# What is moved: the first MLP matmul steps into the pooling mixer, by a generator

## The chip, the cores and the metric

The kernel runs on all 8 cores of one Trainium2 chip, the same program on each: core i takes prompt sequence i (2048 tokens) and 16 of the 128 running sequences (16 x 8 = 128 tokens). No core talks to another. The metric is the device time in microseconds of the slowest core. Each core has TensorE (PE, matmuls into PSUM), VectorE (DVE), ScalarE (ACT), GpSimd (POOL) and SyncE (SP); here POOL and SP issue the DMAs. Every engine works through its own instruction list in the order in which the program wrote it, and waits on semaphores where an operand is not ready.

## The reference, cut to what matters

```python
def trunk(x, c, pool_buf, pos0, ...):
    for i in range(2):                                   # layer 0: pooling mixer, layer 1: spatial gating
        sh1, sc1, g1, sh2, sc2, g2 = split(silu(c) @ w_ada[i] + b_ada[i])     # w_ada[i] is 1024 x 6144
        h = rms_norm(x, norm_g[i, 0]) * (1 + sc1) + sh1
        if i == 0: y, nb = pool_mixer(h, buf, pos0, w_pool, pool_scale)
        else:      y, vr = sgu_mixer(h, ...)
        x = x + g1 * y
        h = rms_norm(x, norm_g[i, 1]) * (1 + sc2) + sh2
        a = relu(h @ mlp_w1[i])                          # 1024 -> 4096
        x = x + g2 * ((a * a) @ mlp_w2[i])               # 4096 -> 1024
    return rms_norm(x, final_g), ...

def pool_mixer(h, buf, ...):
    # four channel groups of 256, windows w = 2, 4, 8, 16:
    # mean of the last w tokens minus the token, then a 256 x 256 map per group, then a scale
    d = mean_w(h) - h
    return einsum('blgc,gcd->blgd', d, w_pool) * pool_scale
```

x is float32, matmul operands are bfloat16.

## The kernel before

Everything is kept transposed, channels on the 128 partitions: x (`xT_sb`) as 8 channel chunks by 2176 tokens in float32 and the normalised h (`hT_sb`) in bfloat16, both whole in SBUF. The tokens are cut into five groups: 0 to 3 are 512 prompt tokens each, group 4 is the 128 sample tokens.

Weights come through a ring of six 128 x 4096 bfloat16 buffers. The list of pieces is fixed: 12 pieces of `w_ada` of layer 0, 12 of layer 1, then for the MLP of layer 0 `w1` and `w2` of block 0, of block 1, and so on (8 blocks of 512 hidden channels). Piece i is loaded by a DMA that POOL issues (L267) as soon as piece i-6 has been used up for the last time.

The stages that matter here, in the order of the program:

- **Front.** Layer 0's modulation (`ada_piece(0, a)`: 32 small matmuls into `psM` and four ACT copies each), and the first norm of the five groups.
- **Pooling mixer**, group by group. DVE builds the eight window sums `dT` of a group (L543 to L564; for group 4 L572 to L586). `mid_group` then puts in the second norm of the group before it: ACT squares x (L350), PE adds the squares up over the channels with a matrix of ones (L353, called the statistics below), DVE and ACT make rstd (L358 to L363), DVE scales x into h (L383), ACT adds the shift (L387). Then come the matmuls of the map, 32 for a group of 512 tokens (L597, L604) into the three banks `psB`, and eight DVE additions into x (L431; L437 and L440 for group 4). After each group `pm_after` uses up three `w_ada` pieces of layer 1, so pieces 9 to 11 come after group 3.
- **MLP of layer 0.** 40 steps, (block, group), blocks outside. `mm1(i)` is 32 matmuls into the three banks `psA` (L459), each bank followed on ACT by relu and square into `aT` (L465, L467). `mm2(i)` is 32 matmuls from `aT` into `psB` (L484) and eight DVE additions into x (L431, or L437 and L440). The order is mm1(0), mm1(1), mm2(0), mm1(2), mm2(1), mm1(3), ... The second norms of groups 3 and 4 are put in behind mm1(0) and mm1(1).
- **Spatial gating and the MLP of layer 1** follow. The gating stage holds three small constants in buffers of their own: `wsp`, `binv`, `btile`.

The window sums of the pooling mixer live in the same two buffers `aT` as the hidden activations of the MLP. A step of the MLP is a pass of the loop in `mlp`; below, step i means mm1(i) followed by mm2(i-1), and "ada pieces" are those of `w_ada`.

Of the kernel before, what the change touches and what calls it, by code (L numbers as in the profile page):

```python
# [134 lines left out]
def build_program():  # L135
# [481 lines left out]
    def sgu_setup():  # L617
        w32 = scr.ap()[:, 0:1024].rearrange("p (g k t) -> p g k t", g=4, k=2)
        m32 = scr.ap()[:, 1024:1280].rearrange("p (k t) -> p k t", k=2)
        S.add("sp", lambda e: e.dma_start(out=w32, in_=d_wsp.ap()), writes=[SCR(0, 4096)], stream="s_wsp")  # L620
# [4 lines left out]
        S.add("pool", lambda e: e.dma_start(out=binv.ap(), in_=d_binv.ap()), writes=[("binv", 0, 1)], stream="s_binv")

    def sgu(after_sub=None, lazy=()):
        l = 1
# [17 lines left out]
        for g, (t0, n) in enumerate(GROUPS):
            c0, _ = hcols(g)
            sample = (g == 4)
# [80 lines left out]
            for cc in range(NDC):
                gi = cc // 2  # L730
                bank, bkey = banks4[nxt("A4", 4)]
                for tt in range(ntile):
# [182 lines left out]
```

How the kernel before makes its waits and increments, by code:

```python
                def body(eng, ops=self.ops[e], e=e):  # L105
                    waited = {}
                    for op in ops:
                        need = {}
                        for d in op.deps:
                            sem, val = d.sigval
                            k = id(sem)
                            if k not in need or need[k][1] < val:
                                need[k] = (sem, val)
                        for k, (sem, val) in need.items():
                            if waited.get(k, 0) >= val:
                                continue
                            eng.wait_ge(sem, val)
                            waited[k] = val
                        ins = op.emit(eng)
                        if op.stream is not None:
                            ins.then_inc(op.sigval[0], 16)
                        elif op.signal:
                            ins.then_inc(op.sigval[0], 1)
                    if e == "sp":
                        for s, (sem, val) in final.items():
                            if waited.get(id(sem), 0) < val:
                                eng.wait_ge(sem, val)
                        for e2 in ENGS:
                            if e2 != e and ecount[e2] > 0:
                                eng.wait_ge(esem[e2], ecount[e2])
```

## Time and profile before

| | us |
|---|---|
| median of 2 runs | 1690.68 (1689.95 to 1691.41) |
| the profiled execution, its own time | 1690.05 |
| its span on core 0, the slowest | 1688.5 |
| spans of the other cores | 1681.3 to 1686.4 |
| PE busy / DVE busy / ACT busy in the span | 1332.7 / 880.4 / 596.0 |

The profile is one execution, recorded on the slowest core. The time around the span is 1690.05 - 1688.5 = 1.55 us. Positions such as "221.49" are microseconds from the start of the span. A matmul of 512 columns is one that streams a group of 512 tokens. A row of the timeline merges neighbouring instructions of one kind ("x31") and gives start and length; what stands in square brackets is the idle time of the engine before it and what ended it. Some matmul records are missing, so that 32 may read as 31.

### The profile page before, as it was taken

The numbers are of one execution on the slowest core, as the hardware profiler recorded it, in microseconds if no ns is written. First come the engines' busy times: TensorE is split into PE (matmuls) and PEld (weight loads), VectorE is DVE, ScalarE is ACT, GpSimd is POOL, SyncE is SP. The second block draws the span as 40 slices with busy tenths as digits, with TensorE's granted clock in tenths as the row PEclk, the third lists the DMA queues.
The fourth block names the chain that finished last, engine by engine and source line by source line (L and its number), as shares of the span: only waits on it lengthen the run. The fifth ranks groups of instructions, "written<-read, shape, count | busy, mean of one in ns | idle before, by whom it ended". The sixth has DMA issues, their size and how long they took to land.

```text
span 1688.5 us, 22112 instructions; the slowest of 8 cores (1681.3 to 1688.5 us)
## 1 busy us (share of the span) xinstructions
PE 1332.7 (79%) x7190; PEld 623.5 (37%) x7314; DVE 880.4 (52%) x1695; ACT 596.0 (35%) x1221; POOL 65.2 (4%) x86
## 2 busy tenths in 40 slices
PE   0233666999999999986888877638999999999982
PEld 0111232444444444432333323323444444444431
DVE  0247775544544435448566466546453544444478
ACT  0450544233233343344412605314334333333352
POOL 2010110000000000000000000000000000000000
PEclk9955777999999999999888978768999999999996
DMA  9999984033123113111200000090311311300023
GB/s 200 200 159 143 144 121 70 1 50 42 20 41 51 25 27 51 26 26 26 57 1 0 1 1 13 7 162 1 51 26 26 51 26 26 51 1 1 1 85 129
DMA packets 75055, 90.05 MB, mean 53 GB/s; under 512 B 4400, under 2 KB 57904, under 8 KB 74928
## 3 DMA queue, kind: packets, MB, share of 16 engines
q0 software_dynamic: 58400, 66.30, 28.0%
q1 hardware_dynamic: 16544, 22.33, 4.4%
q8 instruction: 63, 1.03, 0.3%
q14 instruction: 48, 0.39, 0.1%
HBM read 144.36 MB, written 11.01 MB: 92 GB/s over the span
## 4 chain that ended last, share of the span: by engine, by line
PE 64%; DVE 19%; issue 7%; ACT 4%; DMA 4%; another core or an unknown queue 2%; DVEq 1%; POOL 0%; ACTq 0%; POOLq 0%; SPq 0%
PE psA L459 26%; PE psB L484 26%; PE psB L750 4%; DVE hT_sb L383 4%; DMA ring<-w_ada 3%; PE psS L353 2%; DVE scr L437 2%; DVE xT_sb L440 1%; DVE hT_sb L391 1%; PE psA L659 1%; DVE xT_sb L373 1%; DVE psA L740 1%; DMA btile<-bsp_pack 1%; PE psA L673 1%
## 5 line engine op out<-in xcount | busy, mean ns | idle before, releaser
L431 DVE SCALAR_TENSOR_TENSOR xT_sb<-psB,modT,xT_sb 128x512 f32<-128x512 f32 x544 | 406.1, 750 | 361.0 <-PE psB L484 302.7
L484 PE MATMUL psB<-aT,ring 128*128 128x512 bf16 (+1 forms) x2510 | 500.5, 351 | 59.2 <-DVE scr L437 43.1
L459 PE MATMUL psA<-hT_sb,ring 128*128 128x512 bf16 (+1 forms) x2513 | 485.6, 349 | 9.3 <-ACT aT L465 6.6
L465 ACT ACTIVATE aT<-psA 128x512 bf16<-128x512 f32 (+1 forms) x320 | 169.6, 530 | 608.8 <-PE psA L459 608.6
L484 PEld LDWEIGHTS psB<-aT,ring 128*128 128x128 bf16 x2560 | 233.3, 99 | 315.7 <-issue 80.4
L459 PEld LDWEIGHTS psA<-hT_sb,ring 128*128 128x128 bf16 x2560 | 230.8, 98 | 252.1 <-issue 13.6
L467 ACT ACTIVATE aT<-aT 128x512 bf16<-128x512 bf16 (+1 forms) x320 | 181.1, 566 | 30.4 <-ACT aT L465 1.5
L350 ACT ACTIVATE sq<-xT_sb 128x512 bf16<-128x512 f32 (+1 forms) x200 | 95.3, 558 | 110.7 <-PE psS L353 78.6
L353 PE MATMUL psS<-sq,ones 128*128 128x512 bf16 (+1 forms) x193 | 73.8, 436 | 46.8 <-ACT sq L350 40.9
L295 PE MATMUL psM<-siluT,ring 128*128 128x17 bf16 x768 | 23.5, 173 | 100.5 <-DMA ring<-w_ada 78.9
L383 DVE SCALAR_TENSOR_TENSOR hT_sb<-xT_sb,modT,rstd 128x512 bf16<-128x512 f32 x128 | 92.5, 745 | 9.1 <-ACT rstd L363 9.0
L437 DVE TENSOR_TENSOR scr<-psB,modT 128x128 f32<-128x128 f32 x136 | 39.7, 292 | 103.4 <-PE psB L484 91.2
L750 PE MATMUL psB<-aT,ring 128*128 128x512 bf16 (+1 forms) x312 | 78.8, 415 | 10.9 <-DVE aT L742 9.8
L302 ACT ACTIVATE modT<-psM,vecs_sb 128x17 f32<-128x17 f32 x96 | 18.4, 274 | 140.2 <-PE psM L295 140.2
L597 PE MATMUL psB<-aT,aux4k 128*128 128x512 bf16 (+1 forms) x79 | 29.0, 464 | 48.5 <-DVE xT_sb L431 22.6
L358 DVE TENSOR_SCALAR rstd<-psS 128x512 f32<-128x512 f32 (+1 forms) x25 | 15.2, 608 | 93.6 <-PE psS L353 93.6
L659 PE MATMUL psA<-hT_sb,ring 128*128 128x512 bf16 (+1 forms) x267 | 56.3, 364 | 8.4 <-ACT scr L679 8.0
L295 PEld LDWEIGHTS psM<-siluT,ring 128*128 128x128 bf16 x768 | 22.2, 100 | 103.6 <-issue 102.6
L673 PE MATMUL psA<-ring,hT_sb 128*128 128x512 bf16 x173 | 44.9, 404 | 14.7 <-ACT scr L679 14.4
L353 PEld LDWEIGHTS psS<-sq,ones 128*128 128x128 bf16 x200 | 19.9, 101 | 98.5 <-issue 93.9
L267 POOL DMA_DIRECT2D ring<-mlp_w x32 | 26.9, 840 | 740.0 <-PE psA L459 448.0
L750 PEld LDWEIGHTS psB<-aT,ring 128*128 128x128 bf16 x320 | 34.2, 116 | 54.3 <-issue 34.0
(90 smaller groups left out, 706.4 us busy)
## 6 DMA issues: line engine op xcount, KB each, us to landing
ring<-mlp_w POOLq DMA_DIRECT2D x32, 1024.0 KB, 11.0
ring<-w_ada POOLq DMA_DIRECT2D x24, 1024.0 KB, 42.1
xT_sb<-xT SPq DMA_DIRECT2D x4, 2048.0 KB, 40.9
yT<-xT_sb SPq DMA_DIRECT2D x32, 256.0 KB, 2.0
ring<-sgu_w_in POOLq DMA_DIRECT2D x4, 1024.0 KB, 10.8
ring<-sgu_w_out POOLq DMA_DIRECT2D x2, 1024.0 KB, 13.6
hT_sb<-spT POOLq DMA_DIRECT2D x1, 736.0 KB, 83.7
aux4k<-w_pool POOLq DMA_DIRECT2D x1, 512.0 KB, 77.3
```

What stands on the lines that cost most here:

```text
L350: S.add("act", lambda e, si=si, dc=dc, t0=t0, n=n: e.activation(out=sq[si].ap()[:, 0:n], in_=xT.ap()[:, dc, t0:t0 + n], func=AF.Square), r ...
L353: S.add("pe", lambda e, si=si, dc=dc, n=n: e.matmul(psS.ap()[:, 0:n], ones.ap(), sq[si].ap()[:, 0:n], start=(dc == 0), stop=(dc == NDC - 1 ...
L383: S.add("dve", lambda e, hs=hs, xs=xs, R=R, dc=dc: e.scalar_tensor_tensor(out=hs, in0=xs, scalar=modT.ap()[:, l, DER[vA], dc, 0:1], in1=R, ...
L431: S.add("dve", lambda e: e.scalar_tensor_tensor(out=xs, in0=ps_ap, scalar=modT.ap()[:, l, DER[kG], dout_c, 0:1], in1=xs, op0=ALU.mult, op1 ...
L437: S.add("dve", lambda e: e.tensor_tensor(out=tmp, in0=ps_ap.rearrange("p (b t) -> p b t", t=8), in1=bc_seq(modT.ap(), l, DER[kG], dout_c), ...
L459: S.add("pe", lambda e, pso=pso, wv=wv, dc=dc, fc=fc, c0=c0, n=n: e.matmul(pso, wv[:, dc, fc * 128:(fc + 1) * 128], hT.ap()[:, dc, c0:c0 + n],
L465: S.add("act", lambda e, av=av, pso=pso: e.activation(out=av, in_=pso, func=AF.Relu), reads=[(("psA", bi), 0, 512)], writes=areg)
L467: S.add("act", lambda e, av=av: e.activation(out=av, in_=av, func=AF.Square), reads=areg, writes=areg)
L484: S.add("pe", lambda e, pso=pso, wv=wv, dc=dc, fc=fc, n=n, ab=ab: e.matmul(pso, wv[:, fc, dc * 128:(dc + 1) * 128], aT[ab].ap()[:, fc, 0:n ...
L659: S.add("pe", lambda e, pso=pso, wv=wv, dc=dc, fc=fc: e.matmul(pso, wv[:, dc, (fc % 4) * 128:(fc % 4 + 1) * 128], hT.ap()[:, dc, c0:c0 + n ...
L673: S.add("pe", lambda e, pso=pso, wv=wv, dc=dc, c0=c0, tt=tt: e.matmul(pso, hT.ap()[:, dc, c0 + tt * 128:c0 + (tt + 1) * 128], wv[:, dc, :] ...
L750: S.add("pe", lambda e, pso=pso, wv=wv, dco=dco, cc=cc, uT=uT: e.matmul(pso, wv[:, cc, (dco % 4) * 128:(dco % 4 + 1) * 128], uT[cc], start ...
```

## The change

`mlp` becomes a generator, `mlp_gen`, that yields after each step. It is made before the pooling mixer, and steps of it are drawn in `pm_after`: two behind group 2 (mm1(0); mm1(1) and mm2(0)), one behind group 3 (mm1(2) and mm2(1)), one behind group 4 (mm1(3) and mm2(2)); then comes the second norm of group 4, and then the rest. The second norm of group 3 goes to the middle of group 4 of the mixer, with its shift on ACT. So that window sums and hidden activations can be alive together, the window sums get a buffer of 128 x 4096 bfloat16 of their own, `l1buf`, which later holds `wsp`, `binv` and `btile`.

```diff
-    wsp = sb("wsp", [128, 4, 2, 128], BF16)
-    btile = sb("btile", [128, 4, 128], F32)
-    binv = sb("binv_sb", [1, D], BF16)
+    l1buf = sb("l1buf", [128, 4096], BF16)
...
+    wsp = _V(lambda: l1buf.ap()[:, 0:1024].rearrange("p (g k t) -> p g k t", g=4, k=2))
+    binv = _V(lambda: l1buf.ap()[0:1, 1024:2048])
+    btile = _V(lambda: l1buf.ap()[:, 2048:3072].bitcast(F32).rearrange("p (g t) -> p g t", t=128))
...
-    def mlp(l, after_blk=None, after_last=None, lazy=(), flush=True):
+    def mlp_gen(l, after_blk=None, after_last=None, lazy=(), flush=True):
...
                 mm2(i - 1)
+            yield i
...
-        dT = [aT[0].ap()[:, i, :] for i in range(4)] + [aT[1].ap()[:, i, :] for i in range(4)]
+        dT = [l1buf.ap()[:, i * 512:(i + 1) * 512] for i in range(8)]
...
+    gen0 = mlp_gen(0, after_blk=mlp0_after_blk, after_last=lambda g, part: norm_group(1, 0, g, part=part), lazy=[], flush=False)
+
     def pm_mid(g):
-        if 1 <= g <= 3:
+        if 1 <= g <= 4:
             norm_group(0, 1, g - 1, shift_eng="act")
 
     def pm_after(g):
         for _ in range(3):
             if ada1:
                 ada_piece(1, ada1.pop(0))
+        if g == 2:
+            next(gen0)
+            next(gen0)
+        if g == 3:
+            next(gen0)
...
-    tail0 = mlp(0, after_blk=mlp0_after_blk, after_last=lambda g, part: norm_group(1, 0, g, part=part),
-                lazy=[lambda: norm_group(0, 1, 3), lambda: norm_group(0, 1, 4)], flush=False)
+    next(gen0)
+    norm_group(0, 1, 4)
+    tail0 = run_gen(gen0)
```

What this does to the order on DVE, between groups 2 and 3 of the mixer. Before (L431 is the addition into x, L543 and L549 begin the window sums of group 3):

```order
L358 TENSOR_SCALAR rstd<-psS 128x512
L383 SCALAR_TENSOR_TENSOR hT_sb<-xT_sb,modT,rstd 128x512 x8
L431 SCALAR_TENSOR_TENSOR xT_sb<-psB,modT,xT_sb 128x512 x8
L543 TENSOR_TENSOR aT<-hT_sb 128x512 x2
L549 TENSOR_TENSOR scr<-hT_sb 128x527
```

Now, at the same place (the lines have moved: L439 is the addition, L562 and L568 begin the window sums):

```order
L366 TENSOR_SCALAR rstd<-psS 128x512
L391 SCALAR_TENSOR_TENSOR hT_sb<-xT_sb,modT,rstd 128x512 x8
L439 SCALAR_TENSOR_TENSOR xT_sb<-psB,modT,xT_sb 128x512 x16
L562 TENSOR_TENSOR l1buf<-hT_sb 128x512 x2
L568 TENSOR_TENSOR scr<-hT_sb 128x527
```

The eight additions of mm2(0) stand behind the eight of group 2 and ahead of the window sums of group 3. The same holds behind group 3, with those of mm2(1).

On PE, from the last matmuls of the map of group 3 on. Before (L295 are the ada pieces, L353 the statistics, L459 mm1, L484 mm2):

```order
L604 MATMUL psB<-hT_sb,scr 128x512 x2
L295 MATMUL psM<-siluT,ring 128x17 x96
L597 MATMUL psB<-aT,aux4k 128x128 x16
L459 MATMUL psA<-hT_sb,ring 128x512 x32
L353 MATMUL psS<-sq,ones 128x512 x8
L459 MATMUL psA<-hT_sb,ring 128x512 x32
L353 MATMUL psS<-sq,ones 128x128 x8
L484 MATMUL psB<-aT,ring 128x512 x32
L459 MATMUL psA<-hT_sb,ring 128x512 x32
L484 MATMUL psB<-aT,ring 128x512 x32
L459 MATMUL psA<-hT_sb,ring 128x512 x32
```

Now (L303 the ada pieces, L361 the statistics, L467 mm1, L492 mm2, L616 and L623 the map):

```order
L623 MATMUL psB<-hT_sb,scr 128x512 x2
L303 MATMUL psM<-siluT,ring 128x17 x96
L467 MATMUL psA<-hT_sb,ring 128x512 x32
L492 MATMUL psB<-aT,ring 128x512 x32
L361 MATMUL psS<-sq,ones 128x512 x8
L616 MATMUL psB<-l1buf,aux4k 128x128 x16
L467 MATMUL psA<-hT_sb,ring 128x512 x32
L492 MATMUL psB<-aT,ring 128x512 x32
L361 MATMUL psS<-sq,ones 128x128 x8
L467 MATMUL psA<-hT_sb,ring 128x128 x32
L492 MATMUL psB<-aT,ring 128x512 x32
```

Here mm1(2) and mm2(1) stand ahead of the map of group 4, mm1(3) and mm2(2) behind it, and the statistics of group 4 directly ahead of mm1(4), which is the first matmul step that reads group 4. mm1(0), mm1(1) and mm2(0) stand further up, behind the ada pieces of group 2.

The lists of POOL and SP keep their order: POOL issues the same ring pieces in the same sequence.

## Rows read from the trace of the kernel before

**Rows 1.** Busy time by stretch, core 0: busy us (x instructions) of each engine, granted PE clock, DMA share, GB/s

```profile
200.00:240.00 40.00, 23.16 (x156) 9.71 (x159) 31.99 (x61) 24.44 (x52) 3.38 (x4) 0.76 0.99 131
240.00:280.00 40.00, 28.03 (x188) 12.30 (x189) 21.36 (x70) 14.07 (x33) 2.39 (x3) 0.73 0.74 110
560.00:700.00 140.00, 135.71 (x707) 65.14 (x720) 66.36 (x108) 48.30 (x88) 3.39 (x4) 1.00 0.22 31
220.00:341.00 121.00, 88.36 (x545) 40.51 (x551) 74.10 (x172) 44.53 (x102) 5.80 (x7) 0.82 0.42 57
```

**Rows 2.** Timeline of PE, ada pieces behind groups 2 and 3, map of group 4, mm1(0)

```profile
223.92 0.99 PE L295 MATMUL psM<-siluT,ring 128*128 128x17 bf16 x32 [1.01 <-ACT modT L302]
246.32 0.96 PE L295 MATMUL psM<-siluT,ring 128*128 128x17 bf16 x32
250.25 0.95 PE L295 MATMUL psM<-siluT,ring 128*128 128x17 bf16 x32 [1.01 <-ACT modT L302]
261.11 8.87 PE L459 MATMUL psA<-hT_sb,ring 128*128 128x512 bf16 x31 [0.22 <-issue]
```

**Rows 3.** Timeline of DVE from the window sums of group 3 to those of group 4

```profile
220.92 0.75 DVE L543 TENSOR_TENSOR aT<-hT_sb 128x512 bf16<-128x512 bf16 x2
230.98 0.69 DVE L358 TENSOR_SCALAR rstd<-psS 128x512 f32<-128x512 f32 x1
238.52 2.06 DVE L431 SCALAR_TENSOR_TENSOR xT_sb<-psB,modT,xT_sb 128x512 f32<-128x512 f32 x3
247.26 0.38 DVE L572 TENSOR_TENSOR aT<-hT_sb 128x128 bf16<-128x128 bf16 x2
256.92 0.28 DVE L437 TENSOR_TENSOR scr<-psB,modT 128x128 f32<-128x128 f32 x1
```

**Rows 4.** Timeline, statistics of group 4 to the restart of mm2(0), DVE and PE

```profile
284.90 1.55 PE L353 MATMUL psS<-sq,ones 128*128 128x128 bf16 x8 [1.87 <-ACT sq L350]
287.45 0.28 DVE L358 TENSOR_SCALAR rstd<-psS 128x128 f32<-128x128 f32 x1
288.64 0.29 DVE L399 TENSOR_TENSOR rstd<-xT_sb,modT 128x128 f32<-128x128 f32 x1 [0.91 <-ACT rstd L363]
297.95 2.06 DVE L431 SCALAR_TENSOR_TENSOR xT_sb<-psB,modT,xT_sb 128x512 f32<-128x512 f32 x3
298.84 3.57 PE L484 MATMUL psB<-aT,ring 128*128 128x512 bf16 x8 [8.44 <-DVE xT_sb L431]
```

**Rows 5.** Timeline, the MLP at its pace: steps 2 to 5

```profile
305.06 7.07 PE L459 MATMUL psA<-hT_sb,ring 128*128 128x512 bf16 x32
311.96 7.07 PE L484 MATMUL psB<-aT,ring 128*128 128x512 bf16 x31
313.10 6.79 DVE L431 SCALAR_TENSOR_TENSOR xT_sb<-psB,modT,xT_sb 128x512 f32<-128x512 f32 x8 [7.02 <-PE psB L484]
318.87 7.07 PE L459 MATMUL psA<-hT_sb,ring 128*128 128x512 bf16 x31
332.68 1.95 PE L459 MATMUL psA<-hT_sb,ring 128*128 128x128 bf16 x32
334.68 6.85 PE L484 MATMUL psB<-aT,ring 128*128 128x512 bf16 x31
341.38 7.07 PE L459 MATMUL psA<-hT_sb,ring 128*128 128x512 bf16 x31
```

**Rows 6.** Timeline of POOL: issues of the ring pieces w1(0), w2(0), later w1(3)

```profile
221.49 0.88 POOL L267 DMA_DIRECT2D ring<-mlp_w  x1 [20.33 <-PE psM L295]
223.45 0.75 POOL L267 DMA_DIRECT2D ring<-mlp_w  x1 [1.09 <-PE psM L295]
335.18 0.90 POOL L267 DMA_DIRECT2D ring<-mlp_w  x1 [82.67 <-PE psA L459]
```

**Rows 7.** DMA view, issue to landing (last number, us): the pieces issued at 221.49, 223.45, 335.18

```profile
ring<-mlp_w POOLq DMA_DIRECT2D x1, 1024.0 KB, 15.0
ring<-mlp_w POOLq DMA_DIRECT2D x1, 1024.0 KB, 19.3
ring<-mlp_w POOLq DMA_DIRECT2D x1, 1024.0 KB, 11.6
```

More of the change, by code:

```diff
@@ L185, in build_program, with __init__, ap @@
     siluT = sb("siluT", [128, NDC, NSEQ], BF16)
-    wsp = sb("wsp", [128, 4, 2, 128], BF16)
-    btile = sb("btile", [128, 4, 128], F32)
-    binv = sb("binv_sb", [1, D], BF16)
+    l1buf = sb("l1buf", [128, 4096], BF16)
+    class _V:
+        def __init__(self, f):
+            self.f = f
+        def ap(self):
+            return self.f()
+    wsp = _V(lambda: l1buf.ap()[:, 0:1024].rearrange("p (g k t) -> p g k t", g=4, k=2))
+    binv = _V(lambda: l1buf.ap()[0:1, 1024:2048])
+    btile = _V(lambda: l1buf.ap()[:, 2048:3072].bitcast(F32).rearrange("p (g t) -> p g t", t=128))
     lnst = sb("lnst", [128, 16], F32)
@@ L514, in mlp, with run_gen @@
         return rest_
+    def run_gen(gen):
+        try:
+            while True:
+                next(gen)
+        except StopIteration as e_:
+            return e_.value
+    def mlp(*a_, **k_):
+        return run_gen(mlp_gen(*a_, **k_))
     def pool_mixer(after_group=None, mid_group=None):
@@ L524, in pool_mixer @@
                   reads=[("aux4k", 0, 1)], writes=[SCR(8320 + k_ * 512, 8320 + (k_ + 1) * 512)])
-        dT = [aT[0].ap()[:, i, :] for i in range(4)] + [aT[1].ap()[:, i, :] for i in range(4)]
-        dreg = [[(("aT", 0), i * 512, (i + 1) * 512)] for i in range(4)] + [[(("aT", 1), i * 512, (i + 1) * 512)] for i in range(4)]
+        dT = [l1buf.ap()[:, i * 512:(i + 1) * 512] for i in range(8)]
+        dreg = [[("l1buf", i * 1024, (i + 1) * 1024)] for i in range(8)]
         for g, (t0, n) in enumerate(GROUPS):
@@ L623, in sgu_setup @@
             S.add("dve", lambda e, gi=gi: e.tensor_tensor(out=wsp.ap()[:, gi, :, :], in0=w32[:, gi, :, :], in1=m32, op=ALU.mult),
-                  reads=[SCR(0, 5120)], writes=[("wsp", gi, gi + 1)])
-        S.add("pool", lambda e: e.dma_start(out=binv.ap(), in_=d_binv.ap()), writes=[("binv", 0, 1)], stream="s_binv")
+                  reads=[SCR(0, 5120)], writes=[("l1buf", gi * 512, (gi + 1) * 512)])
+        S.add("pool", lambda e: e.dma_start(out=binv.ap(), in_=d_binv.ap()), writes=[("l1buf", 2048, 4096)], stream="s_binv")
     def sgu(after_sub=None, lazy=()):
@@ L644, in sgu @@
         S.add("sp", lambda e: e.dma_start(out=btile.ap(), in_=bass.AP(d_bsp, 0, [[0, 128], [256, 4], [1, 128]])),
-              writes=[("btile", 0, 1)], stream="s_bt")
+              writes=[("l1buf", 4096, 6144)], stream="s_bt")
         for g, (t0, n) in enumerate(GROUPS):
@@ L677, in sgu @@
                                                                    start=False, stop=True),
-                          reads=[("ones", 0, 1), ("binv", 0, 1)], writes=[(bkey, 0, 512)])
+                          reads=[("ones", 0, 1), ("l1buf", 2048, 4096)], writes=[(bkey, 0, 512)])
                     S.add("act", lambda e, pso=pso, hf=hf: e.activation(out=vst[:, hf * 512:(hf + 1) * 512], in_=pso, func=AF.Gelu,
@@ L727, in sgu @@
                 S.add("sp", lambda e: e.dma_start(out=btile.ap(), in_=bass.AP(d_bsp, 128, [[0, 128], [256, 4], [1, 128]])),
-                      writes=[("btile", 0, 1)], stream="s_bt")
+                      writes=[("l1buf", 4096, 6144)], stream="s_bt")
             for cc in range(NDC):
@@ L735, in sgu @@
                         pso, vtm[:, tt, cc * 128:(cc + 1) * 128], wsp.ap()[:, gi, kk, :], start=True, stop=True),
-                        reads=[SCR(tt * 2048, (tt + 1) * 2048), ("wsp", gi, gi + 1)], writes=[(bkey, 0, 512)])
+                        reads=[SCR(tt * 2048, (tt + 1) * 2048), ("l1buf", gi * 512, (gi + 1) * 512)], writes=[(bkey, 0, 512)])
                 bt = btile.ap()[:, gi, :]
@@ L740, in sgu @@
                 S.add("dve", lambda e, p3=p3, btb=btb: e.tensor_tensor(out=p3, in0=p3, in1=btb, op=ALU.add),
-                      reads=[(bkey, 0, 512), ("btile", 0, 1)], writes=[(bkey, 0, 512)])
+                      reads=[(bkey, 0, 512), ("l1buf", 4096, 6144)], writes=[(bkey, 0, 512)])
                 S.add("dve", lambda e, bank=bank, cc=cc, n=n, uT=uT: e.tensor_tensor(
@@ L813, in build_program, with mlp0_after_blk @@
     ada1 = list(range(12))
+    def mlp0_after_blk(blk):
+        if blk == 6:
+            sgu_setup()
+    gen0 = mlp_gen(0, after_blk=mlp0_after_blk, after_last=lambda g, part: norm_group(1, 0, g, part=part), lazy=[], flush=False)
     def pm_mid(g):
-        if 1 <= g <= 3:
+        if 1 <= g <= 4:
             norm_group(0, 1, g - 1, shift_eng="act")
@@ L829, in build_program @@
     ada_derive_G2(1)
-    def mlp0_after_blk(blk):
-        if blk == 6:
-            sgu_setup()
-    tail0 = mlp(0, after_blk=mlp0_after_blk, after_last=lambda g, part: norm_group(1, 0, g, part=part),
-                lazy=[lambda: norm_group(0, 1, 3), lambda: norm_group(0, 1, 4)], flush=False)
+    next(gen0)
+    norm_group(0, 1, 4)
+    tail0 = run_gen(gen0)
     tail1 = sgu(after_sub=lambda g, part: norm_group(1, 1, g, part=part), lazy=tail0)
```

## The prediction, made blind

> **What bounds the kernel now.** I first read busy time by stretch [rows 1]. From 560 to 700 us the MLP keeps PE busy 135.7 of 140 us at the full clock (1.00, the level of 2.4 GHz): there PE is the bound, nothing of the change touches it, and every microsecond that the MLP starts later goes to the end. From 200 to 280 us it is otherwise: PE 23.2 and 28.0 of 40, DVE 32.0 and 21.4, PE clock 0.76 and 0.73. The engines take turns there. So the change works on a stretch with idle time on PE, some 121 us from 220 to 341, in which PE works 88.4 us and DVE 74.1. Whether the idle time is filled or only moved is then a question of order, and I followed the timeline of DVE and PE through this stretch.
>
> Before, the window sums of group 3 start on DVE at 220.92, its rstd at 230.98, its additions into x at 238.52, and the window sums of group 4 at 247.26 [rows 3]: 26.3 us for a group, of which nearly all is DVE work. MLP step 0 starts on PE at 261.11 [rows 2]. mm2(0) is held up by the second norms of groups 3 and 4 on DVE, restarts at 298.84 after 8.44 us of idle PE [rows 4], and from 305.06 on PE is fed without a gap: mm1(2) 305.06, mm2(1) 311.96, mm1(3) 318.87, mm1(4) 332.68, mm2(3) 334.68, mm1(5) 341.38 [rows 5]. A half step of 512-token width is thus 6.9 us. **The anchor is the start of mm1(5)**, 341.38: from there on both programs are the same, so the shift of this instant is the answer.
>
> **The change, walked through.** The weights decide the first term. w1(0) can only be issued when ada piece 6 of layer 1 is used up; POOL issues it at 221.49 and it lands 15.0 us later, at 236.5 [rows 6, 7]. The last ada piece in front of mm1(0) ends on PE at 224.9 [rows 2]. Before, this landing was hidden: mm1(0) came at 261. Now PE waits from 224.9 to 236.5, 11.6 us. Bounds: the same kind of piece issued alone lands in 11.6 us [rows 7], which would give 233.1; the middle piece of the trio takes 19.3, which would give 240.8. I take 15.0, since the same three pieces go out at the same instants with the same neighbours.
>
> 1. mm1(0) begins after a pause of PE. The same step before took 8.87 us, against 7.07 at the full clock [rows 2, 5]; I take 8.7 start to start: 236.5 to 245.2. mm1(1): 6.9, to 252.1. mm2(0) starts at 252.1 (w2(0), landed at 223.45 + 19.3 = 242.8, is there).
> 2. DVE. Its order says: eight additions of group 2, then eight of mm2(0), then the window sums of group 3. An undisturbed mm2 gives DVE its first bank 1.14 us after PE begins and the eighth addition ends 7.93 us after (311.96, 313.10 + 6.79) [rows 5]. So DVE idles from 220.9 to 253.2, 32.3 us, and is free at 260.0. This is the wait that takes the place of the idle PE: behind it stand the window sums, rstd and the scaling of group 2's norm, and everything of group 3.
> 3. Group 3 takes the 26.3 us it took before: window sums of group 4 would be next at 286.3. Its statistics are on PE by then. PE starts the three ada pieces 0.9 us ahead of that, as before (246.32 against 247.26), and needs 4.9 us (246.32 to 251.2) [rows 2, 3]: 290.3.
> 4. mm1(2) to 297.2, mm2(1) from there, DVE free at 305.1. DVE idled from 286.3 to 298.3 for it.
> 5. Window sums of group 4: 256.92 - 247.26 = 9.7 us, to 314.8. Norm of group 3: 238.52 - 230.98 = 7.5 us, to 322.3. Then the additions of group 4; PE gets to its next step 4.2 us after they begin (261.11 - 256.92), at 326.5 [rows 2, 3].
> 6. mm1(3), after another pause of PE, 8.7 us to 335.2; mm2(2) to 342.1; DVE free at 343.1.
> 7. Norm of group 4, which mm1(4) now waits for with nothing in between. The squares are ready; the statistics, in order on PE behind mm2(2), take about 1.5 us, to 343.6. From rstd to the first scaling 1.2 us, the 24 small operations 297.95 - 288.64 = 9.3 us: 354.2 [rows 4]. mm1(4) runs along, and finishes its other three banks 1.5 us later (2.0 us for four banks, [rows 5]): 355.7. **PE idles some 11 us** here; before, the same 9.3 us of DVE held mm2(0) for 8.4, so this wait isn't taken away but moved.
> 8. mm2(3) 6.7 us, with up to 2 us for a clock that has fallen in the pause: mm1(5) at 362.4 to 364.4.
>
> Against 341.38 that is 21.0 to 23.0 later, **+22 us**. Smaller edits: the shift of group 3's norm goes to ACT and saves DVE eight operations, already in the 7.5 us of step 5. The generator itself and the views into `l1buf` add no instruction. `l1buf` makes `wsp`, `binv` and `btile` wait for the map of group 4, which is over hundreds of microseconds before they are written: nothing, and nothing also if that cover were thinner, as POOL and SP issue them at the same places in their queues. The mask DMA on SP, which waits for the last window sums, slides with them and is needed only from block 6.
>
> The bounds of what the rows of before do not fix, the landing and the restarts of PE at half clock (1.8 us each in steps 1, 6 and 8): 22 - 3.4 - 3 x 1.8 = 13 below, and above, with the late landing and a restart at mm1(2) as well, 22 + 4.3 + 1.8 = 28.
>
> The time goes against the profiled execution: 1690.05 + 22 = 1712. The median of the runs shown, 1690.68, is 0.6 above it, which I leave in the range.
>
> A rule to weigh at the landing. In the rows, w1(0) takes 15.0 us to land while DVE works on bfloat16 sums, and 11.6 us much later, alone in the queue. The Trainium skill (SBUF — State Buffer, section "Who interferes with whom") says that DVE in its two-port modes locks GpSimd out of the port by which it writes the descriptors of its DMAs. Read loosely, an idle DVE would let w1(0) land 3.4 us sooner and the sum would be 18.6. The same section excepts tensor_tensor, which is nearly all that DVE does between 221 and 231, so by the rule as it stands nothing changes.
>
> **Rivals.**
>
> *Early landing.* The trio lands faster beside an idle DVE: 1690.05 + 22 - 3.4 = 1709. For it: DVE is the only thing that changes beside the DMAs. Against: three pieces share the queue either way. It is inside the forecast's own range. With the three restarts at full clock as well the cost is the lower bound, 13: 1703.
>
> *The overlap pays after all (not slower).* One mechanism, at DVE's wait of 32.3 us in step 2: if DVE did group 3's 26.3 us in that gap, and not behind it, the time would be 1712 - 26.3 = 1686, and with the 12 us of step 4 used as well 1674. It decides as soon as 22 us of the two gaps are used. For it: PE's 88.4 us of work in 121 leave room [rows 1], and this is the form the interleaving would need. Against: the order of DVE has the additions of mm2(0) in front of the window sums, and DVE works in order.
>
> *PE stays at half clock.* If the moved half steps all ran at the level of 1.2 GHz, each would take 13.8 us and not 6.9. For the five that I put at full clock (mm1(1), mm2(0), mm1(2), mm2(1), mm2(2)) that is 5 x 6.9 = 34 us more, 1746. Half of it gives 1729, slower by 2.3%. For it: granted clock 0.76 and 0.73 here [rows 1]. Against: mm1(0) itself, after a pause, lost only 1.8 us.
>
> *The change does not do what it says.* The order shows it does; no chance set aside.
>
> **How the numbers follow.** Forecast, 1706 to 1718: 0.75. A lesser cost, 1692 to 1706 (early landing together with short restarts, or a shorter group 3): 0.12. Not slower: 0.04. More than 1718: 0.09, of which above 1724.5 (the +2% line) 0.04. What a measurement of this kernel can tell from no change is about 2%, 34 us; the forecast is 1.3%, so it lies within. The range that should hold the time 8 times in 10 reaches a little below and above the forecast's own: 1703 to 1721. Faster by over 2% (under 1657) needs both gaps used and more: 0.02. Slower by over 2%: 0.04. Within: 0.94.
>
> **What would show it.** In the changed kernel: PE idle between the ada pieces and mm1(0) with w1 as releaser, 11 to 12 us, ending near 236.5; the largest single wait of DVE, some 32 us, at the addition into x, released by a matmul of mm2; the window sums of group 3 near 260, of group 4 near 305; a wait of PE at mm1(4) of 128 columns of about 10 us for h; mm1(5) near 363. The step most apt to fail is the third: if group 3 takes less than 26.3 us because its statistics and matmuls are ready sooner, the cost falls by that much. What would prove it wrong: a mm1(5) before 350, or another stage, behind 350 us, that gains or loses more than 3 us.

## The result, and the profile after

| | before | changed |
|---|---|---|
| median, us | 1690.68, with the later runs 1691.98 | 1715.01 |
| profiled execution, us | 1690.05 | 1712.89 |
| span of its slowest core | 1688.5 (core 0) | 1711.3 (core 3) |
| start of mm1(5) of layer 0 on that core | 341.38 | 364.98 |

The ratio is 1.0135, 95% interval 1.012 to 1.015: slower by 1.35%. Ratios, here and below, leave out the runs in which half of the chip, or all of it, showed a lower granted clock; the medians include them (up to 1844.7 and 1893.7 us here). The forecast was 1712, range 1703 to 1721.

Busy time by stretch on core 3 of the changed kernel, columns as in [rows 1]:

```profile
220.00:341.00 121.00, 74.72 (x446) 33.80 (x447) 57.20 (x128) 47.01 (x97) 4.89 (x6) 0.79 0.37 54
365.00:420.00 55.00, 53.27 (x292) 25.84 (x291) 23.58 (x42) 21.03 (x38) 0.75 (x1) 1.00 0.12 20
```

PE works 74.7 us between 220 and 341 where it worked 88.4, DVE 57.2 where it worked 74.1 [rows 1]. Less is done in the same stretch on both engines, so they wait more, for each other and for weights. From 365 us on PE is at the full clock and nearly always busy, as before.

Some waits between 221 and 363 us, in total, number, longest:

```profile
DVE xT_sb L439 <- PE psB L492: 55.9, 11, 31.2
PE psA L467 <- DMA ring<-mlp_w: 10.2, 1, 10.2
PE psA L467 <- DVE hT_sb L424: 9.0, 8, 2.5
PE psB L616 <- DVE scr L445: 16.7, 5, 14.7
PE psB L616 <- DVE xT_sb L439: 14.2, 1, 14.2
```

The first is DVE at its additions for a bank of mm2, the second PE for w1(0), the third PE at mm1(4) for h of group 4. These are the three waits of the walk. The last two are the other side of the first: PE stands in front of the map of groups 3 and 4 (L616) for 14 us each time, because DVE, freed late from the additions of mm2, has yet to do the norm and to empty the banks. Now the timeline. PE, behind the ada pieces of group 2:

```profile
234.01 16.18 PE L467 MATMUL psA<-hT_sb,ring 128*128 128x512 bf16 x64 [10.18 <-DMA ring<-mlp_w]
250.02 7.07 PE L492 MATMUL psB<-aT,ring 128*128 128x512 bf16 x32
```

PE idles 10.18 us for the ring and starts the two mm1 at 234.01 (before, the first of them came at 261.11 [rows 2]). DVE through groups 3 and 4:

```profile
251.16 6.79 DVE L439 SCALAR_TENSOR_TENSOR xT_sb<-psB,modT,xT_sb 128x512 f32<-128x512 f32 x8 [31.23 <-PE psB L492]
257.87 0.75 DVE L562 TENSOR_TENSOR l1buf<-hT_sb 128x512 bf16<-128x512 bf16 x2
270.15 5.39 DVE L391 SCALAR_TENSOR_TENSOR hT_sb<-xT_sb,modT,rstd 128x512 bf16<-128x512 f32 x8 [1.55 <-ACT rstd L371]
275.46 2.06 DVE L439 SCALAR_TENSOR_TENSOR xT_sb<-psB,modT,xT_sb 128x512 f32<-128x512 f32 x3
297.50 0.75 DVE L439 SCALAR_TENSOR_TENSOR xT_sb<-psB,modT,xT_sb 128x512 f32<-128x512 f32 x1 [13.45 <-PE psB L492]
305.33 0.38 DVE L591 TENSOR_TENSOR l1buf<-hT_sb 128x128 bf16<-128x128 bf16 x2
317.24 5.39 DVE L391 SCALAR_TENSOR_TENSOR hT_sb<-xT_sb,modT,rstd 128x512 bf16<-128x512 f32 x8 [1.56 <-ACT rstd L371]
```

DVE stands still for 31.23 us and then does the additions of mm2(0) at 251.16; only behind them, at 257.87, come the window sums of group 3, which stood at 220.92 before [rows 3]. The second insertion costs it 13.45 us (297.50), and the window sums of group 4 begin at 305.33 against 247.26 [rows 3]. PE again, steps 2 to 5:

```profile
287.78 8.75 PE L467 MATMUL psA<-hT_sb,ring 128*128 128x512 bf16 x32
296.37 8.19 PE L492 MATMUL psB<-aT,ring 128*128 128x512 bf16 x32
326.67 8.21 PE L467 MATMUL psA<-hT_sb,ring 128*128 128x512 bf16 x32
334.71 7.07 PE L492 MATMUL psB<-aT,ring 128*128 128x512 bf16 x32
345.54 0.22 PE L467 MATMUL psA<-hT_sb,ring 128*128 128x128 bf16 x1 [2.54 <-DVE hT_sb L424]
...
353.86 2.83 PE L467 MATMUL psA<-hT_sb,ring 128*128 128x128 bf16 x25 [0.92 <-DVE hT_sb L424]
356.47 8.66 PE L492 MATMUL psB<-aT,ring 128*128 128x512 bf16 x32
364.98 7.07 PE L467 MATMUL psA<-hT_sb,ring 128*128 128x512 bf16 x32
```

mm1(4) of 128 columns runs one matmul for each channel chunk that DVE finishes, from 345.54 to 353.86, and mm1(5) follows at 364.98; in [rows 5] it stood at 341.38. That is 23.6 us later, and the spans differ by 22.8. This sets the slowest core of one profile against the slowest of the other. Core against core, mm1(5) comes 12.7 (core 0) to 28.1 us (core 7) later, 19.9 on average, and the rest of the span behind it changes by -8.9 to +4.5 us, -2.1 on average. Such differences are scatter as far as can be told: on core 1 the same rest differs by 6.8 us between the kernel before and the one below that has only the new buffer. So behind the anchor nothing of weight changed, but agreement to 1 us is more than one profile can show.

### The profile page after: what moved, and what is told of

Read it like the earlier page. It is cut to its first block, busy times and chain, and to the rows that moved or that the text cites. A ratio compares the mean times of both kernels' runs of the same rounds, so it can differ in the third digit from the quotient of the medians.

```text
span 1711.3 us, 22257 instructions; the slowest of 8 cores (1693.4 to 1711.3 us)
## 1 busy us (share of the span) xinstructions
PE 1346.8 (79%) x7314; PEld 626.3 (37%) x7314; DVE 877.7 (51%) x1687; ACT 602.9 (35%) x1229; POOL 65.1 (4%) x86
## 3 DMA queue, kind: packets, MB, share of 16 engines
q0 software_dynamic: 58400, 66.30, 26.7%
## 4 chain that ended last, share of the span: by engine, by line
PE 68%; DVE 16%; issue 6%; DMA 4%; ACT 3%; another core or an unknown queue 1%; DVEq 1%; POOL 0%; ACTq 0%; SPq 0%; POOLq 0%
PE psA L467 27%; PE psB L492 26%; PE psB L769 4%; DVE hT_sb L391 3%; DMA ring<-w_ada 2%; PE psS L361 2%; PE psA L678 2%; PE psA L692 2%; DVE scr L445 2%; DVE xT_sb L448 1%; DVE xT_sb L381 1%; DVE psA L759 1%; DMA l1buf<-bsp_pack 1%; PE psM L692 1%
## 5 line engine op out<-in xcount | busy, mean ns | idle before, releaser
L439 DVE SCALAR_TENSOR_TENSOR xT_sb<-psB,modT,xT_sb 128x512 f32<-128x512 f32 x544 | 406.3, 750 | 399.8 <-PE psB L492 342.1
L492 PE MATMUL psB<-aT,ring 128*128 128x512 bf16 (+1 forms) x2560 | 504.2, 351 | 46.4 <-DVE scr L445 43.0
L467 PE MATMUL psA<-hT_sb,ring 128*128 128x512 bf16 (+1 forms) x2560 | 496.9, 353 | 25.8 <-DMA ring<-mlp_w 10.2
L492 PEld LDWEIGHTS psB<-aT,ring 128*128 128x128 bf16 x2560 | 233.2, 99 | 304.1 <-issue 69.6
L467 PEld LDWEIGHTS psA<-hT_sb,ring 128*128 128x128 bf16 x2560 | 233.5, 99 | 276.5 <-issue 43.2
L361 PE MATMUL psS<-sq,ones 128*128 128x512 bf16 (+1 forms) x200 | 72.8, 425 | 39.1 <-ACT sq L358 31.3
L303 PE MATMUL psM<-siluT,ring 128*128 128x17 bf16 x768 | 23.6, 173 | 98.4 <-DMA ring<-w_ada 76.3
L616 PE MATMUL psB<-l1buf,aux4k 128*128 128x512 bf16 (+1 forms) x80 | 29.5, 461 | 66.7 <-DVE xT_sb L439 30.8
L678 PE MATMUL psA<-hT_sb,ring 128*128 128x512 bf16 (+1 forms) x272 | 56.7, 365 | 8.0 <-ACT scr L698 8.0
L303 PEld LDWEIGHTS psM<-siluT,ring 128*128 128x128 bf16 x768 | 22.3, 100 | 101.7 <-issue 100.7
L366 DVE TENSOR_SCALAR rstd<-psS 128x512 f32<-128x512 f32 (+1 forms) x25 | 15.2, 608 | 81.7 <-PE psS L361 81.7
L361 PEld LDWEIGHTS psS<-sq,ones 128*128 128x128 bf16 x200 | 19.7, 101 | 90.0 <-issue 84.3
```

The lines of the kernel that those rows point to most:

```text
L361: S.add("pe", lambda e, si=si, dc=dc, n=n: e.matmul(psS.ap()[:, 0:n], ones.ap(), sq[si].ap()[:, 0:n], start=(dc == 0), stop=(dc == NDC - 1 ...
L439: S.add("dve", lambda e: e.scalar_tensor_tensor(out=xs, in0=ps_ap, scalar=modT.ap()[:, l, DER[kG], dout_c, 0:1], in1=xs, op0=ALU.mult, op1 ...
L467: S.add("pe", lambda e, pso=pso, wv=wv, dc=dc, fc=fc, c0=c0, n=n: e.matmul(pso, wv[:, dc, fc * 128:(fc + 1) * 128], hT.ap()[:, dc, c0:c0 + n],
L492: S.add("pe", lambda e, pso=pso, wv=wv, dc=dc, fc=fc, n=n, ab=ab: e.matmul(pso, wv[:, fc, dc * 128:(dc + 1) * 128], aT[ab].ap()[:, fc, 0:n ...
L678: S.add("pe", lambda e, pso=pso, wv=wv, dc=dc, fc=fc: e.matmul(pso, wv[:, dc, (fc % 4) * 128:(fc % 4 + 1) * 128], hT.ap()[:, dc, c0:c0 + n ...
```

## The experiments

All times are medians; a ratio is to the kernel before on the same chip, with its 95% interval. The theory (A) is that the time is lost by order alone: weights that have not landed, DVE held by the additions of an inserted step, and PE held by norm 4. Against it stood: the new buffer costs something; the landing wait only replaces another; the half clock of PE sets the stretch; DVE is the bound of the mixer, so that no interleaving can gain.

**Own buffer only.** The steps are no longer drawn into the mixer.

```diff
-        if 1 <= g <= 4:
+        if 1 <= g <= 3:
             norm_group(0, 1, g - 1, shift_eng="act")
...
-        if g == 2:
-            next(gen0)
-            next(gen0)
-        if g == 3:
-            next(gen0)
...
-    next(gen0)
-    norm_group(0, 1, 4)
-    tail0 = run_gen(gen0)
+    tail0 = mlp(0, after_blk=mlp0_after_blk, after_last=lambda g, part: norm_group(1, 0, g, part=part),
+                lazy=[lambda: norm_group(0, 1, 3), lambda: norm_group(0, 1, 4)], flush=False)
```

> The changed kernel with its own buffer for the window sums, but with no step drawn into the mixer (order as before). Theory A (order: the time is lost because DVE and PE wait for each other at the inserted steps): the buffer costs nothing, 1690 to 1692 us, mm1(5) of layer 0 near 341 us. Rival B (the shared buffer and its new dependencies, or other addresses, cost something of their own): 1695 to 1713 us.

1690.73 us, ratio 0.998 (0.996 to 1.001). PE, core 1:

```profile
260.30 9.30 PE L467 MATMUL psA<-hT_sb,ring 128*128 128x512 bf16 x32
340.98 7.07 PE L467 MATMUL psA<-hT_sb,ring 128*128 128x512 bf16 x32
```

The steps stand where they stood in [rows 2, 5], within 1 us. The buffer is free within the interval, and rival B is out: the loss lies in where the steps and the norms of groups 3 and 4 stand. (That the norm of group 3 moved along, with its shift on ACT, was not tested by itself.)

**Weights that have landed.** mm1(0), mm1(1) and mm2(0) read w_ada pieces 11 and 10, which have been in the ring for long. They multiply by the wrong weights, so the kernel's output is not the reference's; only its times are read.

```diff
+            if l == 0 and si < 2:
+                p1 = pidx[("ada", 1, 11)]
+                wv = pview(p1)
...
+            if l == 0 and si < 1:
+                p2 = pidx[("ada", 1, 10)]
+                wv = ring[p2 % NS].ap()[:, 0:4096].rearrange("p (a b) -> p a b", b=1024)
```

> The changed kernel, but mm1(0), mm1(1) and mm2(0) of layer 0 read ring pieces of w_ada that have landed long before (so the product of these steps is not the reference's); same instructions, same order. Theory A with the landing as its first term: mm1(0) starts at 225 us right behind the ada pieces on every core, the wait of 10 us for the ring is gone, the restart at half clock too; on the slowest core mm1(5) moves from 365 to about 353 and the time is 1701 us (1697 to 1704). Rival C (the landing only takes the place of another wait, PE being held up elsewhere anyway): at most 3 us better than the changed kernel, 1710 to 1715.

1704.01 us, ratio 1.007 (1.005 to 1.009): 11.0 less than the changed kernel, where 14 were expected. There are only four runs, and three of them took 1701.67, 1701.87 and 1706.16 us, so the 11 is good to some 4 us. PE, core 0 (the mm1 are L470 here, mm2 L498):

```profile
223.54 14.92 PE L470 MATMUL psA<-hT_sb,ring 128*128 128x512 bf16 x62 [0.23 <-issue]
238.30 7.07 PE L498 MATMUL psB<-aT,ring 128*128 128x512 bf16 x32
351.97 7.07 PE L470 MATMUL psA<-hT_sb,ring 128*128 128x512 bf16 x31
```

mm1(0) starts at 223.54, with no wait in front, and mm1(5) at 351.97, as walked (353). The median came out at the upper edge of the range. So the landing is worth some 11 us on the slowest core: a real term, and not another wait in disguise (rival C is out). Averaged over the cores it is less: mm1(0) starts 7.4 us earlier than in the changed kernel (224.5 against 231.8), and mm1(5) 7.4 us earlier too. What is left, 12 us over before, must come from the order behind it; the next runs take that apart.

**Norm 4 ahead of step 3.**

```diff
-    next(gen0)
     norm_group(0, 1, 4)
+    next(gen0)
     tail0 = run_gen(gen0)
```

> The changed kernel with the second norm of group 4 put ahead of step 3 and not behind it. Theory A: mm1(3) starts about 5 us later because the statistics stand in front of it, but the 24 small DVE operations run beside mm1(3) and PE no longer idles at mm1(4); mm1(5) about 9 us earlier than in the changed kernel, near 355, time 1704 to 1707. Rival D (the wait is only moved to mm2(2), as it stood at mm2(0) before the change): no more than 3 us better, 1710 to 1715.

1705.42 us, ratio 1.0085 (1.0065 to 1.0105): 9.6 less than the changed kernel. PE, core 6:

```profile
331.50 1.91 PE L467 MATMUL psA<-hT_sb,ring 128*128 128x512 bf16 x4
339.90 2.75 PE L492 MATMUL psB<-aT,ring 128*128 128x512 bf16 x12
344.99 6.03 PE L492 MATMUL psB<-aT,ring 128*128 128x512 bf16 x19 [2.33 <-DVE xT_sb L439]
350.86 1.95 PE L467 MATMUL psA<-hT_sb,ring 128*128 128x128 bf16 x32
359.55 7.07 PE L467 MATMUL psA<-hT_sb,ring 128*128 128x512 bf16 x31
```

mm1(4) comes at 350.86 in one piece, without the trickle. Rival D is out, since more than 3 us were gained, but it is right in a small part: mm2(2) waits 2.33 us for DVE, which ends norm 4 at 344.1. Here core 6 got its weights late (mm1(0) at 238.8), so mm1(5) at 359.55 and not 355.

**Draws behind the window sums.**

```diff
     def pm_mid(g):
+        if g == 3:
+            next(gen0)
+            next(gen0)
+        if g == 4:
+            next(gen0)
         if 1 <= g <= 4:
             norm_group(0, 1, g - 1, shift_eng="act")
...
-        if g == 2:
-            next(gen0)
-            next(gen0)
-        if g == 3:
-            next(gen0)
```

> The changed kernel with the steps drawn one place later: step 0 and 1 behind the window sums of group 3 (not ahead of them), step 2 behind those of group 4. Theory A (DVE's waits of 31 and 13 us at the additions of mm2 hold up the window sums): the sums, 10 us each, now lie in the gaps; PE's order and the landing stay as they are. 8 to 9 us less at each place, mm1(5) near 348, time 1695 to 1699. Rival E (it is PE's late start and its half clock that set the stretch, and DVE's order doesn't matter): within 3 us of the changed kernel.

1699.46 us, ratio 1.0044 (1.0034 to 1.0054): 15.6 less, half a us above the range expected, with PE's order of half steps as it was and the landing too (on this core PE waits 11.67 us for w1(0) and starts mm1(0) at 234.74). DVE, core 0:

```profile
219.07 0.75 DVE L562 TENSOR_TENSOR l1buf<-hT_sb 128x512 bf16<-128x512 bf16 x2
251.79 6.80 DVE L439 SCALAR_TENSOR_TENSOR xT_sb<-psB,modT,xT_sb 128x512 f32<-128x512 f32 x8 [22.57 <-PE psB L492]
262.58 5.39 DVE L391 SCALAR_TENSOR_TENSOR hT_sb<-xT_sb,modT,rstd 128x512 bf16<-128x512 f32 x8 [1.55 <-ACT rstd L371]
289.92 6.78 DVE L439 SCALAR_TENSOR_TENSOR xT_sb<-psB,modT,xT_sb 128x512 f32<-128x512 f32 x8 [3.78 <-PE psB L492]
300.69 5.39 DVE L391 SCALAR_TENSOR_TENSOR hT_sb<-xT_sb,modT,rstd 128x512 bf16<-128x512 f32 x8 [1.54 <-ACT rstd L371]
```

The window sums of group 3 start at 219.07, inside the gap, and the longest wait falls from 31.23 to 22.57 us, the second from 13.45 to 3.78. The scaling of norm 2 comes at 262.58 where it came at 270.15, that of norm 3 at 300.69 where it came at 317.24. Rival E is out: DVE's order does matter, some 8 us per place.

**Each draw one group later.**

```diff
-        if g == 2:
+        if g == 3:
             next(gen0)
-            next(gen0)
-        if g == 3:
             next(gen0)
...
+    next(gen0)
     next(gen0)
     norm_group(0, 1, 4)
```

> The changed kernel with every draw one group later: steps 0 and 1 behind group 3, steps 2 and 3 behind group 4, then the second norm of group 4. The weights have landed by then. Theory A: no wait for the ring; DVE still waits 19 us for mm2(0) behind group 3 (two mm1 and a bank after 252 us) and PE still idles 11 us at mm1(4); mm1(5) near 345 us, time 1694 to 1697. Rival C (the landing is not what the draw behind group 2 costs, each inserted step costs the same wherever it stands): 1705 or more.

1696.84 us, ratio 1.0031 (1.0017 to 1.0045). PE, core 6:

```profile
254.45 15.66 PE L467 MATMUL psA<-hT_sb,ring 128*128 128x512 bf16 x64
298.77 9.00 PE L467 MATMUL psA<-hT_sb,ring 128*128 128x512 bf16 x32
332.26 0.22 PE L467 MATMUL psA<-hT_sb,ring 128*128 128x128 bf16 x1 [2.54 <-DVE hT_sb L424]
350.32 7.07 PE L467 MATMUL psA<-hT_sb,ring 128*128 128x512 bf16 x32
```

mm1(0) follows the ada pieces with nothing in between. 18.2 us of the changed kernel's loss thus hang on the draws standing one group too early; this run moves the landing and DVE's order together and doesn't divide them. Rival C (1705 or more) is out again. mm1(5) comes at 350.32, above my 345: this core reached its ada pieces 3.4 us later than core 0 did before (249.70 against 246.32 [rows 2]), and mm1(2) at 298.77 took 9.0 us. PE still gets h of group 4 chunk by chunk, from 332.26 on.

**Both repairs in one kernel**: draws behind the window sums, norm 4 ahead of step 3 (the two diffs above).

> Both single repairs in one kernel: draws behind the window sums, and the second norm of group 4 ahead of step 3. Theory A: the two waits lie at different places, so the gains add up: 1699.5 - 9.6 = 1690, 1688 to 1693, level with the kernel before; what is left against an ideal overlap is the landing and mm2(0) standing in front of norm and map of group 3. Rival F (the gains overlap): 1695 or more.

1689.70 us, ratio 0.9987 (0.998 to 0.9997): level with before, to 0.2%. The gains add, 9.6 + 15.6 = 25.2 from 1715.0 gives 1689.8, and rival F is out.

The slowest core mixes these gains with how early its weights landed. The time from the start of mm1(0) to the start of mm1(5) leaves the landing out. In one profiled execution of each kernel, over the eight cores:

| kernel | mm1(0) to mm1(5), us, mean (lowest to highest) |
|---|---|
| changed | 128.0 (126.5 to 131.0) |
| landed weights | 128.0 (126.6 to 128.9) |
| norm 4 ahead | 121.6 (120.7 to 123.0) |
| draws behind the window sums | 112.8 (111.9 to 113.6) |
| both | 104.9 (104.3 to 106.1) |

So norm 4 is worth 6.4 us by this measure, less than the 9.6 of the medians, the draws 15.2, and both together 23.1. The single repairs, with the 11 us of the landing, come to 36 us, more than the 23 that were lost. They are no shares of that loss: the kernel before had waits of its own here (8.44 us of PE at mm2(0) [rows 4]), and a kernel with all three repairs was not run.

**Only mm1 in the mixer.** mm1 uses PE and ACT but no DVE. The generator also yields behind mm1. So mm1(0) comes behind the map of group 3, mm1(1) ahead of the map of group 4 (the first of the two draws there only ends step 0), mm2(0) behind that map, and mm1(2), mm2(1) and mm1(3) with a w_ada piece behind each.

```diff
                 mm1(i)
+                yield i
...
         if 1 <= g <= 4:
             norm_group(0, 1, g - 1, shift_eng="act")
+        if g == 4:
+            next(gen0)
+            next(gen0)
...
         for _ in range(3):
-            if ada1:
+            if g < 3:
                 ada_piece(1, ada1.pop(0))
-        if g == 2:
-            next(gen0)
-            next(gen0)
         if g == 3:
             next(gen0)
     pool_mixer(after_group=pm_after, mid_group=pm_mid)
+    next(gen0)
+    norm_group(0, 1, 4)
     while ada1:
+        next(gen0)
         ada_piece(1, ada1.pop(0))
...
-    next(gen0)
-    norm_group(0, 1, 4)
     tail0 = run_gen(gen0)
```

> Only mm1, which needs no DVE, is put into the mixer: mm1(0) behind the map of group 3, mm1(1) ahead of the map of group 4, mm2(0) behind it; the second norm of group 4 behind mm2(0); the last three ada pieces between later half steps. Own buffer for the window sums as in the change. Theory A (what costs is DVE waiting for PE and PE for weights and norm, each inserted half step that makes nobody wait is a gain): the weights of 236 us are there at 246, DVE waits some 2 us for statistics, mm2(0) at 270 us, mm1(5) near 318 us, time 1667 (1664 to 1672), 2 us for each us uncertain in PE's restart. Rival G (interleaving cannot gain since DVE is the bound of the mixer): 1688 or more.

1678.72 us, ratio 0.9933 (0.991 to 0.996): faster than both kernels, so rival G is out, but 12 us short of what I expected. PE, core 0:

```profile
246.51 7.07 PE L467 MATMUL psA<-hT_sb,ring 128*128 128x512 bf16 x32
259.68 6.45 PE L467 MATMUL psA<-hT_sb,ring 128*128 128x512 bf16 x24
269.07 3.39 PE L467 MATMUL psA<-hT_sb,ring 128*128 128x512 bf16 x8 [2.95 <-ACT aT L473]
277.08 9.67 PE L492 MATMUL psB<-aT,ring 128*128 128x512 bf16 x32 [0.42 <-DVE scr L445]
299.49 4.48 PE L492 MATMUL psB<-aT,ring 128*128 128x512 bf16 x20 [1.21 <-DVE xT_sb L439]
327.92 7.07 PE L467 MATMUL psA<-hT_sb,ring 128*128 128x512 bf16 x32
```

mm1(0) came where it should (246.51). Its neighbour mm1(1) did not: of its four banks the last had to wait 2.95 us for ACT, which was adding the shift of norm 3 to h and let the banks of mm1(1) stand. The map of group 4 stands behind on PE, and DVE waits for it:

```profile
272.68 0.29 DVE L445 TENSOR_TENSOR scr<-psB,modT 128x128 f32<-128x128 f32 x1 [5.05 <-PE psB L617]
```

mm2(0) then runs at half clock in part (9.67 us for 32 matmuls against 7.07 at the full clock; granted clock 0.73 from 277 to 287 us). I had also left the three ada pieces (some 3 us) and the 1.21 us at 299.49 out of the sum.

**ACT's order.** mm1(1) goes between the statistics of norm 3 and its scaling, so that ACT empties its banks first; the shift isn't needed before mm1(3).

```diff
-        if 1 <= g <= 4:
+        if 1 <= g <= 3:
             norm_group(0, 1, g - 1, shift_eng="act")
         if g == 4:
+            norm_group(0, 1, 3, part="stats")
             next(gen0)
             next(gen0)
+            norm_group(0, 1, 3, part="mod", shift_eng="act")
```

> As the kernel that puts only mm1 into the mixer (1678.7 us), but in group 4 mm1(1) stands between the statistics of norm 3 and its scaling, so that ACT empties the banks of mm1(1) before it adds the shift to h of group 3. In the run before, the fourth bank of mm1(1) waited 2.95 us for ACT and DVE then 5.05 us for the map of group 4. Theory A: these two waits fall by 4 to 5 us together, nothing else moves, 1674 us (1672 to 1676). Rival H (PE's half clock, not ACT's order, holds the map up): within 1.5 us of 1678.7.

1674.44 us, ratio 0.988 (0.981 to 0.996), with the next kernel the fastest of the study: 16.8 below the runs of before around it, 40.6 below the changed kernel. It is 4.3 below the kernel above. The intervals of the two ratios overlap, but three of its four runs (1673.70 to 1674.80 us) lie below all four of that kernel (1676.39 to 1682.46), and in the profiles mm1(5) starts at 319.3 to 322.1 us on the eight cores, against 324.9 to 328.0. Rival H is out. PE, core 6:

```profile
257.71 8.16 PE L467 MATMUL psA<-hT_sb,ring 128*128 128x512 bf16 x31
270.49 8.57 PE L492 MATMUL psB<-aT,ring 128*128 128x512 bf16 x31 [0.52 <-DVE scr L445]
320.25 7.07 PE L467 MATMUL psA<-hT_sb,ring 128*128 128x512 bf16 x31
```

mm1(1) is in one piece, mm2(0) at 270.49 instead of 277.08 (the core is 2.0 us ahead: 4.6 us net), mm1(5) at 320.25.

**The last ada pieces in PE's gap of group 3.**

```diff
+        if g == 3:
+            norm_group(0, 1, 2, part="stats")
+            while ada1:
+                ada_piece(1, ada1.pop(0))
+            norm_group(0, 1, 2, part="mod", shift_eng="act")
```

> The same, and the last three ada pieces go between the statistics of norm 2 and the map of group 3, where PE idles 6 us for DVE. Theory A: their 3 us of PE between the later half steps go, PE comes warmer to the map of group 3 (whose additions waited 0.8 to 1 us each), against 1 us of delay of its first bank: 2 to 4 us less than the kernel with the ACT order alone, near 1671 (1668 to 1674). Rival: the pieces hold up the map by as much as they free, no gain.

1675.68 us, ratio 0.988 (0.979 to 0.998): no gain over the ACT order alone (three of its five runs took 1673.21 to 1675.68 us), so the rival holds, though its reason is another. PE, core 0 (the two waits are the same on all eight cores, within 0.01 us):

```profile
234.74 0.99 PE L303 MATMUL psM<-siluT,ring 128*128 128x17 bf16 x32 [2.45 <-ACT modT L310]
289.00 2.75 PE L492 MATMUL psB<-aT,ring 128*128 128x512 bf16 x11
296.66 6.13 PE L492 MATMUL psB<-aT,ring 128*128 128x512 bf16 x20 [4.91 <-DVE xT_sb L439]
```

The pieces do fit in the gap (one of them, at 234.74, waits 2.45 us for ACT). But with mm1(2) following mm2(0) closely and no piece between it and mm2(1), PE is at mm2(1) before DVE has ended norm 4, and waits 4.91 us instead of 1.21. What was freed turned into a new wait. mm1(5) comes at 322.5 to 327.0 us on the eight cores, not earlier than with the ACT order alone; why the whole time is level all the same stays open.

## Why the prediction was right

The forecast was +22 us and 1712; measured 1715.0, and in the profiled execution +22.8 us. Step by step, forecast and core 3:

| step | forecast | trace |
|---|---|---|
| 1: PE waits for w1(0) | 11.6, to 236.5 | 10.2, to 234.0 |
| 1: mm1(0) and mm1(1) together | 15.6 | 16.0 |
| 2: DVE idle in front of mm2(0) | 32.3 | 31.2 |
| 2: DVE free for group 3 | 260.0 | 257.9 |
| 3: group 3 on DVE | 26.3 | 26.2 (to 281.58 + 2.48) |
| 4: mm1(2) and mm2(1) together | 13.8 | 16.6 |
| 5: window sums of group 4 | 305.1 | 305.3 |
| 6: mm1(3) | 326.5 | 326.7 |
| 7: mm2(3) | 355.7 | 356.5 |
| 8: mm1(5) | 362.4 to 364.4 | 365.0 |

Two terms were mis-sized and cancelled. Core 3 was about 2 us ahead up to step 3; and in step 4 I let mm1(2) run at the full clock, though it stands behind the small ada matmuls and a pause. It took 8.75 us (granted clock 0.79 from 288 to 296), mm2(1) 8.19. I had that restart only in the upper bound.

Part of the close agreement is luck. I worked the sum out on core 0, the slowest before, with its landing of 15.0 us. In the changed kernel core 0 had its weights in 8.6 us and mm1(5) came only 12.7 us later there. The 22 us hold because another core was late instead: core 3, whose w1(0) took 13.5 us, and which before stood 3.1 us ahead of core 0 (mm1(5) at 338.30) and so lost 26.7 of its own. The same waits stand in the trace of every core; that their price on the slowest core would be near 22 rested on some core landing late.

The rule weighed at the landing (SBUF — State Buffer, "Who interferes with whom"): with DVE idle from 219.9 us, w1(0) took 13.5 us to land on core 3 (issue 220.41), against 15.0 on core 0 before. That is no clean test, as the last section shows that the cores differ by more among themselves. The mean over the eight cores went from 11.7 to 11.0 us, so the rows show no sign of the 3.4 us that the loose reading would give, in agreement with the exception for tensor_tensor. The "early landing" rival is what happened on half of the cores (8.6 to 9.1 us), though not by way of the idle DVE, which all of them had; the metric takes the other half.

The overlap rival named the place where it would be decided, DVE's order at the first insertion. The draws behind the window sums used 8.7 of the 31.2 us there and 9.7 of the 13.5 at the second, and the kernel with only mm1 in the mixer came out on that rival's side of the line. The half-clock rival fell: on core 3 the moved half steps mm2(0) and mm2(2) took 7.07 us, as at the full clock, mm1(0) with mm1(1) 16.0 and not 27.6, and mm1(2) and mm2(1) together 2.8 us more than the full clock gives; the granted clock was 0.79 from 220 to 341 against 0.82.

What stays open: mm2(1) on core 3 had a granted clock of 0.83 from 297 to 304 us with matmuls evenly spaced (DVE's additions, one for four matmuls, start 1.05 us apart and not 0.86), while core 4 shows 1.00 there. I didn't pursue it.

## What to carry to other kernels

An idle engine is filled only by work that the engines beside it needn't wait for. Before a step is moved up, walk down the list of every engine it touches and ask what stands behind it there: here PE had the room, but the step ended in eight DVE additions, and on DVE 10 us of window sums and all that hangs on them stood behind these. DVE had idle time too, 31 us of it; what it lacked was an order that let it use it. Split such a step at that border, move the half that needs only the idle engine, and put it where its data have landed; then look at the next engine in the chain (ACT here), since its order decides whether the moved half leaves the buffers in time.

## What the runs showed of the hardware that was not expected

A landing can differ by half between two cores of a pair. mm1(0) and mm1(1) of the changed kernel, PE on cores 1, 2 and 5:

```profile
233.85 16.10 PE L467 MATMUL psA<-hT_sb,ring 128*128 128x512 bf16 x64 [9.61 <-DMA ring<-mlp_w]
228.10 16.11 PE L467 MATMUL psA<-hT_sb,ring 128*128 128x512 bf16 x64 [5.75 <-DMA ring<-mlp_w]
228.63 15.86 PE L467 MATMUL psA<-hT_sb,ring 128*128 128x512 bf16 x64 [5.52 <-DMA ring<-mlp_w]
```

In each of the pairs 0-1, 2-3, 4-5, 6-7 one core got w1(0) in 8.6 to 9.1 us and the other in 12.9 to 13.5 (issue to landing: 8.6 and 12.9, 9.1 and 13.5, 8.8 and 13.5, 8.6 and 13.1). The spans follow the landings: 1698.7, 1699.7, 1694.2, 1693.4 us on the early cores, 1706.0, 1711.3, 1704.4, 1708.2 on the late ones. Before, the landings were as uneven (9.2 to 15.0 us) but hidden, and the spans lay within 7.2 us of each other. In all four pairs, before and after, the early core is the one that issued first, counted from its own first instruction; in the changed kernel by 1.5 to 4.4 us, so the later issue is a part of what the late core loses. With landed weights in the three half steps the spans lie within 7.5 us of each other again, so it is the exposed wait that spreads them. The Trainium skill (HBM Reference, "Specifications (TRN2)") says that the two cores of a pair share the bandwidth of their HBM. The rows don't contradict that, but they don't show it either: no run here had one core load alone, and what makes one core of a pair late stays open. For a kernel timed by its slowest core, an exposed wait for a DMA costs what the late core pays.
